# Hybrid conv / MLA / mixture-of-experts step: normed rows in three buffers, other load places for the first expert matrices

## The reference

```
p = x @ w_in -> conv branch, MLA attention branch, two gates
mix = (sigmoid(g_conv) * y_conv + sigmoid(g_attn) * y_attn) @ w_o
h   = layernorm(ALPHA * x + mix, ln1_g, ln1_b)
lg  = h @ router_w_group;  grp = argmax            # 4 groups
le  = h @ router_w_expert; top 2 of 8 inside grp   # 32 experts
for each expert e, for the rows routed to it:
    y += w * ((silu(h @ w_gate[e]) * (h @ w_up[e])) @ w_down[e])
out = layernorm(ALPHA * h + y, ln2_g, ln2_b)
```

## Time and profile before

| | |
|---|---|
| median of 3 runs | 1737.98 us |
| the profiled execution, own time | 1735.35 us |
| its span in the profile | 1733.6 us |
| PE (matmul) busy | 1650.6 us, 95% |
| PEld (weight load) busy | 1014.1 us |
| DVE busy | 661.6 us, 38% |
| ACT busy | 339.5 us, 20% |
| POOL busy | 163.6 us, 9% |
| DMA moved | 337.67 MB |
| mean granted TensorE clock | 0.975 |

### The profile page before, as it was taken

One profiled execution on the slowest core, in us unless ns is written; L12 is line 12 of the kernel. 1 busy time (PEld: TensorE's weight loads), 2 busy tenths in 40 slices (PEclk: granted clock), 3 DMA queues, 4 the chain that ended last, 5 costly groups with the idle time before them and its releaser, 6 DMA issues.

```text
span 1733.6 us, 22526 instructions
## 1 busy us (share of the span) xinstructions
PE 1650.6 (95%) x9287; PEld 1014.1 (58%) x9288; DVE 661.6 (38%) x1395; ACT 339.5 (20%) x670; POOL 163.6 (9%) x169
## 2 busy tenths in 40 slices
PE   8999999999999999999999999889999999999890
PEld 5557777777776666666688455544444444444440
DVE  1446454545442323232577654541112221211225
ACT  1112222223231222222212000011111111111115
POOL 1000000000003321121000000001111111111110
PEclk9999999999999999999899999889999999999995
DMA  7200121211117554342452521599999999999975
GB/s 230 58 21 20 49 62 49 62 49 50 46 41 208 192 172 136 122 161 84 155 191 74 221 97 73 140 269 396 394 389 384 386 407 381 387 382 386 388 279 201
DMA packets 104554, 337.67 MB, mean 195 GB/s; under 512 B 24522, under 2 KB 68626, under 8 KB 88068
## 3 DMA queue, kind: packets, MB, share of 16 engines
q1 hardware_dynamic: 89716, 276.22, 43.1%
q0 software_dynamic: 13568, 55.78, 10.7%
q10 hardware_dynamic: 1168, 4.23, 0.6%
HBM read 307.90 MB, written 35.51 MB: 198 GB/s over the span
## 4 chain that ended last, share of the span: by engine, by line
PE 84%; DMA 11%; DVE 2%; issue 1%; ACT 1%; another core or an unknown queue 0%; SPq 0%; POOL 0%; DVEq 0%; POOLq 0%; ACTq 0%
PE psum L1068 12%; PE psum L1182 9%; DMA arena<-in_w_up 8%; PE psum L1513 6%; PE psum L1370 6%; PE psum L1508 6%; PE psum L1385 5%; PE psum L1534 4%; PE psum L1109 4%; PE psum L972 3%; PE psum L1221 3%; PE psum L1540 2%; PE psum L1082 2%; PE psum L1521 2%; PE psum L1127 2%; PE psum L1116 2%
## 5 line engine op out<-in xcount | busy, mean ns | idle before, releaser
L1068 PE MATMUL psum<-arena 128*128 128x258 f32 x896 | 215.3, 384 | 0.0
L1182 PE MATMUL psum<-arena 128*128 128x344 f32 x576 | 184.0, 461 | 0.0
L1068 PEld LDWEIGHTS psum<-arena 128*128 128x128 f32 x896 | 162.8, 190 | 27.9 <-issue 7.0
L1508 PE MATMUL psum<-arena 128*128 128x512 f32 x320 | 141.5, 600 | 1.1 <-DVE arena L2540 1.1
L1514 PE MATMUL psum<-arena 128*64 128x512 f32 x320 | 141.6, 595 | 0.0
L1513 PE MATMUL psum<-arena 128*64 128x512 f32 x320 | 141.6, 595 | 0.0
L1182 PEld LDWEIGHTS psum<-arena 128*128 128x128 f32 x576 | 104.1, 191 | 53.8 <-issue 12.6
L1508 PEld LDWEIGHTS psum<-arena 128*128 128x128 f32 x320 | 60.7, 192 | 74.7 <-issue 74.2
L1370 PE MATMUL psum<-arena 128*128 128x258 f32 x448 | 100.0, 387 | 0.9 <-ACT arena L1795 0.9
L1385 PE MATMUL psum<-arena 128*128 128x512 f32 x224 | 99.2, 596 | 0.0
L1370 PEld LDWEIGHTS psum<-arena 128*128 128x128 f32 x448 | 86.7, 194 | 14.3 <-issue 1.3
(11 more groups left out here) (394 smaller groups left out, 2133.2 us busy)
## 6 DMA issues: line engine op xcount, KB each, us to landing
arena<-in_w_gate SPq DMA_DIRECT2D x31, 2048.0 KB, 28.7
arena<-in_w_up SPq DMA_DIRECT2D x31, 2048.0 KB, 34.0
arena<-in_w_down SPq DMA_DIRECT2D x31, 2048.0 KB, 38.0
arena<-in_w_in SPq DMA_DIRECT2D x33, 512.0 KB, 4.2
gates<-arena SPq DMA_DIRECT2D x16, 516.0 KB, 6.0
arena<-gates SPq DMA_DIRECT2D x16, 516.0 KB, 6.1
arena<-in_x_prompt SPq DMA_DIRECT2D x16, 512.0 KB, 4.5
arena<-in_w_o SPq DMA_DIRECT2D x1, 4096.0 KB, 17.6
```

The source lines that it names most:

```text
L1068: ins = mm(psum[:, BANK[name[0]], 0:QT], held, moved, start=(k == 0 and name in ("X1", "V6", "Y5")), stop=(k == 3), skip_group_check=True)
L1182: ins = mm(psum[:, FB + t, 0:SP3], wring[:, u, k, :], xT[:, k, t * SP3:(t + 1) * SP3], start=(k == 0), stop=(k == KD - 1))
L1508: ins = mm(psum[:, bank, :], xgT[:, xpar, k, :], w[:, k, :], start=(k == 0), stop=(k == KD - 1))
```

## The change

The norm stage writes its tiles in turn into three buffers (`h_ring`, `h_of(n)` is buffer n % 3) instead of `h_sb`; VectorE waits before it overwrites a buffer until both writes of the tile three before have landed. Three semaphores each count the landings of `h_rows` and of `sums`, in place of one and two. The one-hot rows of the first two experts lie in columns of `mT`. The ring's places are numbered otherwise: 3 and 4 are the region at the start of the arena, 5 to 7 are the last three of the big zone. Matrices 3 and 4 are issued in the norm stage, behind the rows of tile n = 2 and of n = 4; matrix 5 after the last router. All are whole transfers. Matrices 0 to 7 go to places 0 to 7, and the later ones follow the order of `AGAIN`: 8 and 9 take places 0 and 1 and wait for expert 0's gate and up; 10 and 11 take places 8 and 9 behind the slot tables; from 12 on a matrix again takes the place of the one ten before. TensorE issues ten filling matmuls instead of four at L1499.

```diff
-        h_sb = at(Z0, NT, D)
...
-        oh_fixed = z(NT, SOON, P)
+        h_ring = [at(Z0 + 2 * KD * FE, D), z(D), z(D)]
+
+        def oh_fixed(n):
+            t = max(n, 1) - 1
+            return mT[:, 2:4, t * P:(t + 1) * P] if n else mT[:, 4:6, t * P:(t + 1) * P]
+
+        def h_of(n):
+            return h_ring[n % 3]
...
-        ring_at = [Z3 + i * MAT for i in range(6)] + [Z0, Z0 + MAT, Z3 - 64 - 2 * MAT, Z3 - 64 - MAT]
+        ring_at = [Z3, Z3 + MAT, Z3 + 2 * MAT, Z0, Z0 + MAT, Z3 + 3 * MAT, Z3 + 4 * MAT, Z3 + 5 * MAT, Z3 - 64 - 2 * MAT, Z3 - 64 - MAT]
...
+        AGAIN = (0, 1, 8, 9, 2, 3, 4, 5, 6, 7)
...
+        def place(j):
+            return j if j < 8 else AGAIN[(j - 8) % RING]
+
+        def earlier(j):
+            return [i for i in range(j) if place(i) == place(j)]
...
             def load_matrix(j, e):
-                if j >= RING:
-                    n, m = divmod(j - RING, 3)
+                if earlier(j):
+                    n, m = divmod(earlier(j)[-1], 3)
                     sp.wait_ge((g_done, u_done, d_done)[m], n + 1)
-                sp.dma_start(ring(j), matrix(j % 3, e)).then_inc(we_ld[j % RING], 16)
-            def load_parts(j, e):
-                for c in range(4):
-                    part = slice(32 * c, 32 * c + 32)
-                    sp.dma_start(ring(j)[part], matrix(j % 3, e)[part]).then_inc(we_ld[j % RING], 16)
+                elif place(j) >= 8:
+                    sp.wait_ge(ws_dve, 1)
+                sp.dma_start(ring(j), matrix(j % 3, e)).then_inc(we_ld[place(j)], 16)
             for m in range(3):
                 load_matrix(m, 0)
             for n, t in enumerate(TILE):
                 sp.wait_ge(h_dve, n + 1)
-                sp.dma_start(h_rows[t * P:t * P + rows_of(t), :], h_sb[0:rows_of(t), t, :]).then_inc(h_out, 16)
+                sp.dma_start(h_rows[t * P:t * P + rows_of(t), :], h_of(n)[0:rows_of(t)]).then_inc(h_out[n % 3], 16)
                 if n + 3 < NT:
                     load_residual(n + 3)
+                if n in (2, 4):
+                    load_matrix(2 + n // 2, 1)
             sp.wait_ge(lg_done, NT)
             sp.wait_ge(h_dve, NT)
-            for m in range(2):
-                load_parts(3 + m, 1)
-            sp.wait_ge(tb_done, 1)
-            load_parts(5, 1)
...
+            load_matrix(5, 1)
...
-            e = expert_at(2)
-            load_matrix(6, e)
-            load_matrix(7, e)
-            sp.wait_ge(ws_dve, 1)
-            load_matrix(8, e)
-            for n in range(3, NE):
+            for n in range(SOON, NE):
                 e = expert_at(n)
                 for m in range(3):
                     load_matrix(3 * n + m, e)
...
             mm(psum[:, 2, 0:NE + 1], more_w[0:NE], tri[0:NE, 0:NE + 1], start=True, stop=True).then_inc(pos_done, 1)
-            keep_busy(4, 1)
+            keep_busy(10, 1)
...
+                if n >= 3:
+                    dve.wait_ge(h_out[n % 3], H_BASE[n % 3] + 16 * (n // 3))
+                    dve.wait_ge(ah_out[n % 3], A_BASE[n % 3] + 16 * (n // 3))
-                stt(out=h_sb[0:r, t, :], in0=v, scalar=rsm[0:r, s, 2:3], in1=ln1b[0:r], op0=ALU.mult, op1=ALU.add).then_inc(h_dve, 1)
+                stt(out=h_of(n)[0:r], in0=v, scalar=rsm[0:r, s, 2:3], in1=ln1b[0:r], op0=ALU.mult, op1=ALU.add).then_inc(h_dve, 1)
```

More of the change, by code:

```diff
@@ L248, in build @@
         row_f2, blk_f = z(2, NT), z(2, NT)
-        fin = h_sb
+        fin = at(Z0, NT, D)
         ln2g, ln2b = at(ring_at[9], D), at(ring_at[9] + D, D)
@@ L386, in build @@
         wo_done, r_dve, var_dve, sd_act = sem("wo_done"), sem("r_dve"), sem("var_dve"), sem("sd_act")
-        h_dve, h_out = sem("h_dve"), sem("h_out")
+        h_dve = sem("h_dve")
+        h_out, H_BASE = wconv_ld, (16 * 4,) * 3
+        ah_out, A_BASE = gate_out, GATE_OUT
         ht_done, ht_act, lg_done, lg_dve = sem("ht_done"), sem("ht_act"), sem("lg_done"), sem("lg_dve")
@@ L398, in build @@
         we_ld = [sem(f"we_ld{i}") for i in range(6)] + wgate_ld
-        WE_BASE = [0] * 3 + [48] * 3 + [16 * (NH // 2 + KD // 2)] * 4
+        WE_BASE = [0] * 6 + [16 * (NH // 2 + KD // 2)] * 4
         ord_dve = sem("ord_dve")
@@ L523, in rest_at @@
             return P // 2 if three(n) else 0
+        def place(j):
+            return j if j < 8 else AGAIN[(j - 8) % RING]
+        def earlier(j):
+            return [i for i in range(j) if place(i) == place(j)]
         def ring(j):
-            v = at(ring_at[j % RING], MAT)
+            v = at(ring_at[place(j)], MAT)
             return v.rearrange("p (k n) -> p k n", n=D if j % 3 == 2 else FE)
         def landed(j):
-            return WE_BASE[j % RING] + 16 * (j // RING + 1)
+            return WE_BASE[place(j)] + 16 * (len(earlier(j)) + 1)
         w_in = a["w_in"][0].rearrange("(k p) n -> p k n", p=P)
@@ L756, in _ @@
                 sp.wait_ge(h_dve, n + 1)
-                sp.dma_start(h_rows[t * P:t * P + rows_of(t), :], h_sb[0:rows_of(t), t, :]).then_inc(h_out, 16)
+                sp.dma_start(h_rows[t * P:t * P + rows_of(t), :], h_of(n)[0:rows_of(t)]).then_inc(h_out[n % 3], 16)
                 if n + 3 < NT:
                     load_residual(n + 3)
+                if n in (2, 4):
+                    load_matrix(2 + n // 2, 1)
             sp.wait_ge(lg_done, NT)
             sp.wait_ge(h_dve, NT)
-            for m in range(2):
-                load_parts(3 + m, 1)
-            sp.wait_ge(tb_done, 1)
-            load_parts(5, 1)
-            sp.wait_ge(h_out, 16 * NT)
-            for q in range(2):
-                sp.wait_ge(ah_out[q], 16 * ((NT - q + 1) // 2))
+            load_matrix(5, 1)
+            for q in range(3):
+                sp.wait_ge(h_out[q], H_BASE[q] + 16 * (NT // 3))
+                sp.wait_ge(ah_out[q], A_BASE[q] + 16 * (NT // 3))
             sp.wait_ge(ord_dve, 1)
@@ L904, in _ @@
             pool.wait_ge(ht_done, 1)
-            pool.wait_ge(h_out, 16 * NT)
-            for q in range(2):
-                pool.wait_ge(ah_out[q], 16 * ((NT - q + 1) // 2))
+            for q in range(3):
+                pool.wait_ge(h_out[q], H_BASE[q] + 16 * (NT // 3))
+                pool.wait_ge(ah_out[q], A_BASE[q] + 16 * (NT // 3))
             pool.memset(xg, 0.0).then_inc(xg_clear, 1)
@@ L1413, in turn_h @@
                         pe.wait_ge(h_dve, NT)
-                    ins = nc.tensor.transpose(psum[:, 4 + k // 4, (k % 4) * P:(k % 4) * P + r], h_sb[0:r, TILE[n], k * P:(k + 1) * P], ident[0:r, 0:r])
+                    ins = nc.tensor.transpose(psum[:, 4 + k // 4, (k % 4) * P:(k % 4) * P + r], h_of(n)[0:r, k * P:(k + 1) * P], ident[0:r, 0:r])
                     if n == NT - 1 and k == KD // 2 - 1:
@@ L1441, in first_table @@
                 for k in range(SOON):
-                    ins = mm(psum[:, 2 + k, 0:1], oh_fixed[:, n, k, :], tok_f[:, n:n + 1], start=(n == 0), stop=(n == NT - 1))
+                    ins = mm(psum[:, 2 + k, 0:1], oh_fixed(n)[:, k, :], tok_f[:, n:n + 1], start=(n == 0), stop=(n == NT - 1))
                 if n == NT - 1:
@@ L1558, in gate_up @@
             def gate_up(n):
-                pe.wait_ge(we_ld[3 * n % RING], landed(3 * n))
+                pe.wait_ge(we_ld[place(3 * n)], landed(3 * n))
                 pe.wait_ge(te_act, n + 1)
@@ L1565, in gate_up @@
                     up(2, ring(3 * n), n % 2).then_inc(g_done, 1)
-                    pe.wait_ge(we_ld[(3 * n + 1) % RING], landed(3 * n + 1))
+                    pe.wait_ge(we_ld[place(3 * n + 1)], landed(3 * n + 1))
                     pe.wait_ge(hu_dve, n)
@@ L1584, in down_proj @@
             def down_proj(n):
-                pe.wait_ge(we_ld[(3 * n + 2) % RING], landed(3 * n + 2))
+                pe.wait_ge(we_ld[place(3 * n + 2)], landed(3 * n + 2))
                 pe.wait_ge(th_act, n + 1)
@@ L1825, in _ @@
                 ins.then_inc(ht_act, 1)
-                if n >= 2:
-                    act.wait_ge(ah_out[n % 2], 16 * (n // 2))
+                if n >= 3:
+                    act.wait_ge(ah_out[n % 3], A_BASE[n % 3] + 16 * (n // 3))
                 act.wait_ge(h_dve, n + 1)
-                act.dma_start(sums[t * P:t * P + r, :], h_sb[0:r, t, :]).then_inc(ah_out[n % 2], 16)
+                act.dma_start(sums[t * P:t * P + r, :], h_of(n)[0:r]).then_inc(ah_out[n % 3], 16)
             act.wait_ge(sel_dve, ABOVE)
@@ L2427, in norm_last @@
                 link(nc.vector.reciprocal(rsm[:, s, 2:3], rsm[:, s, 1:2]))
+                dve.wait_ge(h_out[n % 3], H_BASE[n % 3] + 16 * (n // 3))
+                dve.wait_ge(ah_out[n % 3], A_BASE[n % 3] + 16 * (n // 3))
                 for c in range(2):
                     half = slice(c * 512, (c + 1) * 512)
-                    stt(out=h_sb[:, t, half], in0=v[:, half], scalar=rsm[:, s, 2:3], in1=ln1b[:, half], op0=ALU.mult, op1=ALU.add).then_inc((h_half, h_dve)[c], 1)
```

(3 more changed lines are left out.)

1 line of the change is left out of this document (removed).

## The result

The changed kernel takes 1727.55 us, the median of 4 runs (1724.58 to 1728.96); the kernel before had 1738.91 (1737.29 to 1740.34, 4 runs) beside it. The ratio is 0.9933, 95% interval 0.9915 to 0.9950: 11.6 us less (8.7 to 14.8). Forecast were 7.3 less, 1730.7 us, in a range of 1723.5 to 1737. The profiled execution took 1724.58 us, its span is 1722.8: 10.8 us under the one of before. The causes are looked for in these two executions, and then tested on medians and ratios.

A forecast was written before the change was run, and what follows sets the result against it. From about 1380 us TensorE follows the stream of weights (6.05 us a matrix). Matrix 82 ahead by 7.4 less 0.1 for the norm stage gives 7.3 us, so 1730.7 us on the median of 1737.98; range 1723.5 to 1737.

The forecast's parts named there:

- 5.9 + 1.5: Lead at matrix 82: TensorE ahead by 5.9 us from an earlier expert 0, its waits for up matrices 1.5 us shorter.
- Norm stage: Stage before the experts: two matrices loaded early hold nobody up; costed at +0.1 us (0 to 0.5).
- The first gather: Gather of rows before expert 0: takes 8 to 11 us beside one whole matrix, landing at 1121 to 1124.5.
- the gather stays late: Rival, 13%: matrices 6 and 7 delay the first gather, expert 0 starts at 1130.15 again; time 1733.9 us.
- the use I had for the Trainium skill: Rule on GpSimd descriptors and VectorE's shared port: the 16.7 us gather would come from VectorE; judged little supported by the trace.
- Ten fillers end at 1127: Before expert 0: filling matmuls, not the gather, release it at 1127, 3.15 us before the 1130.15 of now.
- The clock came back at 1123.0: TensorE's return to full clock during the fillers: 4.5 calls done by then, 5.5 following at 0.7 us.
- The ring: Weight buffer places: matrix 12 issued at 1171.0 into an empty queue, landed at 1181.1; stream ahead by 7.4 us.
- Not by the 4.19 MB loaded early: Weight stream: ahead by 7.4 us, not the 10 us of the early load, as the ring limits it in between.
- Waits 9.9: TensorE's waits for up matrices fall from 11.4 to 9.9 us; the last stays 4.4 us, low clock behind it too.
- the rival on the slow side: Rival, 8%: the pace of the weights worsens after the idle time at 1163 to 1171; at 6.2 us, 1741.2.
- the waits vanish: Rival, 8%: stream pace 5.9 instead of 6.05 us, so 9.9 us of waits and 2.2 of low clock go; 1718.6.

## Why the prediction was right, and where it was off

**Direction and mechanism: right.** The gain was to come from an earlier expert 0 and an earlier stream, whose sum is the lead of matrix 82. It did: 8.3 + 2.6 where 5.9 + 1.5 stood.

**Norm stage, +0.1 (0 to 0.5): no cost seen.** Both matrices go in among the tiles, VectorE has no wait for a write of rows in its list of 995 to 1112, and the first row shown of the seam is 0.24 us earlier (1107.89 for 1108.13). No run shows the 0.1 of the sum: in the last tile VectorE's reciprocal and the write behind it, between which the two new waits stand, start 0.20 us apart in both traces (1101.92 and 1102.12 before, 1101.47 and 1101.67 after).

**The first gather, 8 to 11 us: wrong, 3.3.** I bounded it from below by the shortest gather of before, 6.9, and no row there showed one with DMA nearly free. The runs give three: 3.2 and 3.3 behind one matrix, 11.0 behind three whole ones, 16.6 behind three in quarters. It did no harm, since I had the fillers, not the gather, release expert 0; the kernel with four fillers (transposes 3.2 us earlier, still without a wait) confirms that. The rival "the gather stays late" falls. With it falls the use I had for the Trainium skill, SBUF — State Buffer (section "SBUF: two separate sides"): VectorE was busy for 2.18 of the 3.5 us in which this gather was set up and landed, and it landed in 3.3; those small operations did not hold it. (In the kernel before they did not run all through the gather's set-up either, as I wrote: VectorE was idle from 1112.56 to 1114.41.) Whether the page's rule holds for operations of the kind that it names, no run here shows.

**Ten fillers end at 1127: this is the step that was mis-sized.** They ended at 1124.5. "The clock came back at 1123.0" was taken over from the trace of before as if it were a date; TensorE had worked there from 1108 to 1122.3 much as after, yet after it came back at 1119.6. That is 3.4 us more at full clock, of which the fillers took 2 us. The other 0.46 us is their start, 1116.35 for 1116.81. So TensorE is ahead by 5.67 at the transposes (3.15 forecast), 0.92 in them and 1.72 in the first up: 8.3. That is a little over the 3 to 8 I gave this lead. In the repeat of the change the clock came back at 1123.8 and the transposes started at 1128.1: so far does this term spread with the form of the seam, which I can't predict.

**The ring.** The issues moved as forecast, by TensorE's lead: 8 at 1133.7 (about 1136 forecast), 9 at 1140.7 (1143), 10 and 11 at 1147 (1149), 12 at 1168.6 (1171.0), 15 at 1184.2 (1186.6). The gap was forecast for 1163 to 1171 and was at 1162 to 1169. The stream gained 2.6 over TensorE instead of 1.5; the old order of places, with 2 to 4 us more in time and 10.5 us of waits, shows what it comes from. The 1.1 us between arises at the restart of the stream behind the gap and not in its later pace: matrix 19 already landed at 1218.9 for 1229.6, 10.7 us ahead. One size in it was wrong: with the 10.1 and 6.05 of the forecast matrix 13 would have landed 16.15 us after the issue of 12, at 1184.8, and it landed at 1182.9 (issued at 1169.1, 13.8 to landing). Another was rough: before, matrices 15 to 19 landed 5.75 us apart (1206.6 and 1229.6), not 6.05 and not 5.96 at best, which makes the 1188.5 for matrix 12 an estimate only. How the 1.1 divides stays open. "Not by the 4.19 MB loaded early: the ring is the limit in between" held in three runs: loading 3 and 4 late costs nothing measurable, and moving or cutting 12 to 14 gains 1 to 4 us instead of the 8 to 11 that bandwidth would give. Here my own expectation after the result was worse than the prediction: for both of those runs I had forgotten matrix 15.

**Waits 9.9, the last one unchanged: nearly right.** 8.8, and 4.3 at last with the low clock behind it. The pace of the weights did not get worse (the rival on the slow side), nor did the waits vanish.

**What made the gain**, from single edits: whole transfers 5.0 us (of 11.6, or 9.6 in the repeat), the order of places about 3, the rest, mainly the early load and ten fillers together, about 2 (0.9958 against 0.9971). Only the first is clear of the noise; the other two are sizes whose intervals overlap. The early load and the fillers work against each other: the early load makes the gather short, and the ten fillers then last longer than it. Without fillers, and with the places as freed, the early load is worth about 7.

## What to carry to other kernels

A prefetch that starts earlier pays only up to the next place in its buffer: before moving loads, list for each later load which consumer frees its place and when, and let each load take the place that is freed next (here 5 to 8 us of 1727, for no more memory). When a wait is covered by filling work, recount the filling as soon as the wait gets shorter. And split a load by partitions only after looking at its GB/s.

## What the hardware showed that I had not expected

- Loads in quarters of 32 partitions ran at 202 GB/s with all DMA engines busy, whole ones at 413 and up to 430 after. By the Trainium skill, SBUF — State Buffer (section "Door 1: The DMA port swizzle"), 32 neighbouring partitions reach only half of the 16 ports; by that rule the quarters run at half rate, and the trace agrees. I had read both numbers and not priced the rate by itself.
- In the kernel before with ten fillers the clock (1.00 from 1125.2 to 1131.8) was back at its low level from 1132 on, within the wait of 3.58 us that followed the fillers. Filling that ended before the wait did was wasted here.
- The seam comes in two forms. In the early one the clock is low for short stretches only and is back between 1116.6 and 1123.0; in the late one it is at 0.50 without a break, from some 1098 to 1102 on until about 1122 at the earliest. In the repeated change it is so though TensorE is busy for 20.86 of 23.5 us, and expert 0 starts 3.7 us later than in the change:

```profile
1100.00:1123.50 23.50, 20.86 (x70) 15.63 (x70) 10.29 (x47) 2.13 (x3) 3.82 (x3) 0.50 0.50 173
1124.20:1130.00 5.80, 4.98 (x21) 3.12 (x19) 0.72 (x2) 0.77 (x2) 0.00 (x0) 1.00 0.99 424
```

These are stretches of the repeated change. Of the fourteen profiled executions seven have each form. Both forms occur in the same kernel (the change and its repeat). What decides between them stays open.
